# Two-layer decoder trunk on one core: the last two experts' rows spread over the tokens by TensorE instead of stored and loaded again

## The reference

```python
h = rms_norm(x, norm_ffn_w[layer])
# router: the best of 4 groups, then the best 2 of its 4 experts; weights e_w
gates = sum(one_hot(expert_id, 16) * e_w)            # 2 of 16 are non-zero per token
gu = einsum('nd,edf->nef', xt, w_gate_up)            # 16 experts, 1024 x 512
act = silu(gate) * up * gates
x = x + einsum('nef,efd->nd', act, w_down)           # 256 x 1024
```

## Time and profile before

| | us |
|---|---|
| runs | 1179.62, 1181.15, 1185.16 (median 1181.15) |
| profiled execution, its own time | 1181.09 |
| profiled execution, span | 1179.3 |
| PE busy | 1111.8 (94%) |
| DVE busy | 701.5 (59%) |
| ACT busy | 608.6 (52%) |
| POOL busy | 405.1 (34%) |
| DMA bytes | 194.76 MB, mean 165 GB/s |

### The profile page before, as it was taken

The page is one execution under the profiler, slowest core; times in us unless marked ns, Lnnn a source line. Parts: engine busy times, 40 slices in busy tenths (PEclk is TensorE's granted clock), DMA queues, the critical chain, the costliest instruction groups (busy, mean ns, idle before and its releaser), DMA issues.

```text
span 1179.3 us, 19724 instructions
## 1 busy us (share of the span) xinstructions
PE 1111.8 (94%) x7062; PEld 912.1 (77%) x7063; DVE 701.5 (59%) x1016; ACT 608.6 (52%) x903; POOL 405.1 (34%) x344
## 2 busy tenths in 40 slices
PE   8999999999998899998999999999999997999980
PEld 5778887778787688886788888888888886888870
DVE  5435444367736999996646341543442138999975
ACT  5556234242434699995633342233342234899871
POOL 4343121110133244442155325442244442344442
PEclk8999999999999899999999999999999997999995
DMA  9333311112225699996443213331222364999955
GB/s 262 79 86 56 72 38 55 37 44 66 72 68 210 244 353 375 379 364 238 174 128 98 81 56 106 97 106 56 81 73 91 104 190 161 354 388 374 358 208 223
DMA packets 89859, 194.76 MB, mean 165 GB/s; under 512 B 20348, under 2 KB 21432, under 8 KB 89016
## 3 DMA queue, kind: packets, MB, share of 16 engines
q1 hardware_dynamic: 67560, 159.34, 40.6%
q10 hardware_dynamic: 12432, 17.60, 4.4%
q0 software_dynamic: 9792, 16.80, 3.8%
HBM read 189.50 MB, written 23.07 MB: 180 GB/s over the span
## 4 chain that ended last, share of the span: by engine, by line
PE 80%; DVE 8%; DMA 5%; ACT 3%; issue 2%; ACTq 1%; SPq 0%; POOL 0%; POOLq 0%; DVEq 0%
PE ps L674 23%; PE ps L676 22%; PE ps L675 22%; PE ps L2570 2%; PE ps L2362 2%; DMA raw<-in_moe_w_down_dram 1%; DMA arena<-y 1%; DVE x L1467 1%; PE ps L2245 1%; ACTq L1421 1%; PE ps L2498 1%; DMA arena<-hs,slot_rows 1%; PE ps L2199 1%; ACT wh L1007 1%; DMA y<-arena,cur_rows 1%
## 5 line engine op out<-in xcount | busy, mean ns | idle before, releaser
L841 POOL TENSOR_TENSOR wl<-raw,wh 128x1024 fp32r<-128x1024 f32 x94 | 228.6, 2440 | 380.5 <-ACT wh L1007 380.2
L674 PE MATMUL ps<-wh,hT_hi 128*128 128x512 f32 x864 | 346.7, 401 | 3.5 <-DVE hT_lo L1986 2.4
L676 PE MATMUL ps<-wh,hT_lo 128*128 128x512 f32 x864 | 337.9, 391 | 0.0
L675 PE MATMUL ps<-wl,hT_hi 128*128 128x512 f32 x864 | 337.2, 390 | 0.0
L1007 ACT ACTIVATE wh<-raw 128x1024 fp32r<-128x1024 f32 x116 | 122.4, 1068 | 212.6 <-PE ps L676 191.0
L674 PEld LDWEIGHTS ps<-wh,hT_hi 128*128 128x128 f32 x864 | 162.8, 188 | 39.1 <-issue 3.5
L676 PEld LDWEIGHTS ps<-wh,hT_lo 128*128 128x128 f32 x864 | 162.3, 188 | 34.6
L675 PEld LDWEIGHTS ps<-wl,hT_hi 128*128 128x128 f32 x864 | 162.8, 188 | 30.9
L674 PE MATMUL ps<-hT_hi,wh 128*128 128x512 f32 (+1 forms) x296 | 116.9, 395 | 2.1 <-DVE arena_rounded L1818 1.0
L1961 DVE TENSOR_TENSOR wl<-arena,wh 128x1024 fp32r<-128x1024 f32 x96 | 113.8, 1222 | 4.7 <-ACT wh L1294 3.1
L1961 DVE TENSOR_TENSOR wl<-raw,wh 128x1024 fp32r<-128x1024 f32 x92 | 109.5, 1223 | 8.2 <-ACT wh L1294 5.4
(11 more groups left out here) (331 smaller groups left out, 1576.8 us busy)
## 6 DMA issues: line engine op xcount, KB each, us to landing
raw<-in_moe_w_gate_up_dram SPq DMA_DIRECT2D x64, 512.0 KB, 11.5
arena<-in_moe_w_gate_up_dram SPq DMA_DIRECT2D x64, 512.0 KB, 10.5
raw<-in_odd_w_in_dram SPq DMA_DIRECT2D x48, 512.0 KB, 3.7
raw<-in_even_w_in_dram SPq DMA_DIRECT2D x32, 512.0 KB, 4.8
arena<-in_moe_w_down_dram SPq DMA_DIRECT2D x32, 512.0 KB, 11.7
raw<-in_moe_w_down_dram SPq DMA_DIRECT2D x32, 512.0 KB, 14.1
raw<-in_odd_w_out_dram SPq DMA_DIRECT2D x16, 512.0 KB, 3.6
arena<-y ACTq DMA_DIRECT2D x6, 1024.0 KB, 9.9
```

Source lines behind the costliest of these rows:

```text
L674: nc.tensor.matmul(dst, lh, rh, start=first, stop=False)
L675: nc.tensor.matmul(dst, lh, rl, start=False, stop=False)
L676: return nc.tensor.matmul(dst, ll, rh, start=False, stop=last)
L841: pool.tensor_tensor(columns_of(i, wl[:, i % NSPL, :, :]), raw_columns(i), columns_of(i, wh[:, i % NSPL, :, :]).bitcast(F32), ALU.subtract ...
```

## The change

The last two experts (14 and 15, `LAST = NE - 2`) are no longer scattered to `y2`. What changes, part by part:

- ACT multiplies their results by the slot's weight while it copies them out of PSUM (`late_hi`, rounded), DVE makes the low part (`late_low`), and PE adds them to token tiles with a 0/1 matrix per expert (`slot_token`, 128 slots x 512 tokens): 8 matmuls of 128 x 512 for each token tile (`late_rows`). DVE adds the PSUM result to `X` (`add_late`).
- The matrices are made on DVE after its part of expert 0 (`slot_tokens`, two instructions of 128 x 512), from numbers made at the end of `pair_weights` (five more small instructions).
- The slots' weights: ACT stores the pair weights to DRAM after expert 1 (`w_dram`, 512 runs of 8 bytes), POOL gathers them by slot with two indirect DMAs. POOL also scatters rows of zeros to the pair rows of experts 14 and 15, by two indirect DMAs, so that the combines can go on over all of `y2`, with those pairs' weight set to 0 (`w_early`). The four stand after the first two experts' turn on POOL (`late_experts`).
- The five loads of `y2` are issued by SP, behind the first four pieces of the next layer, as soon as expert 13's scatter has landed.
- Order in `norm(2)` and `norm(4)` on DVE: two combines of tile 0, `late_low` of expert 15, then combines and `add_late` alternate. In `norm(2)` the low parts of layer 1's first two pieces go to POOL, the two others come after `lo_tiles` of tile 0. `keep_busy` is gone from PE; `late_rows` stand in its place and between the tiles.
- One more memset of 128 x 1024 (`no_rows`) in `outnorm` of each layer.
- The overflow branch is adapted.

```diff
-    return i in DVE_LO or ... or first_piece(10) <= i < first_piece(10) + 4
+    return i in DVE_LO or ... or first_piece(10) + 2 <= i < first_piece(10) + 4
 # SP
+            def load_early_rows(l):
+                for q in range(2):
+                    sp.wait_ge(s_(f"y_stored{q}"), 112 * (l + 1))
+                sp.wait_ge(s_("late_ready"), 64 * (l + 1))
+                sp.wait_ge(s_("slot_token_made"), 2 * (l + 1))
+                ...
+                sp.dma_start(YP[0][:, 0, :], src[0][:, 0, :]).then_inc(s_("yp_loaded0"), 16)
+                sp.dma_start(YP[0][:, 1, :], src[0][:, 1, :]).then_inc(s_("yp_second0"), 16)
+                for T in range(1, NT):
+                    sp.dma_start(YP[T], src[T]).then_inc(s_(f"yp_loaded{T}"), 16)
             for i in range(after, after + 4):
                 load(i)
+            load_early_rows(0)
             overflow_sp(sp, 0)
-            sp.wait_ge(s_("yp_loaded3"), 16)
 # POOL, between two_experts(0) and the loop
+                def late_experts():
+                    pool.wait_ge(s_("w_stored"), 16 * (l + 1))
+                    for e in range(2):
+                        ... indirect_dma_start(out=w_slot[:, e:e + 1], in_=w_dram[l], by rows) -> late_ready
+                    for e in range(2):
+                        ... indirect_dma_start(out=y2_dram[l], by rows, in_=no_rows) -> late_ready
 # ACT
+                    if last and par == 1:
+                        hi(m + 6 * NE)
+                        hi(m + 6 * NE + 1)
                     act.wait_ge(s_("ysb_free"), E + 1)
+                        if last:
+                            act.activation(late_hi[:, par, c], ps[:, 2 + hf, :], ACT.Copy, scale=w_slot[:, par:par + 1])...
+                            continue
+                    if n == 1:
+                        act.wait_ge(s_("slot_token_made"), 2 * (l + 1))
+                        act.dma_start(w_dram[l] ..., v3(w12, 4)).then_inc(s_("w_stored"), 16)
-                for q in range(2):
-                    act.wait_ge(s_(f"y_stored{q}"), 128 * (l + 1))
-                act.dma_start(YP[:, 0, 0, :], src[0][:, 0, :])...   # and the four others
 # DVE
+            def late_low(l, e, hf):
+                stt(late_lo[:, e, c], ps[:, 2 + hf, :], w_slot[:, e:e + 1], late_hi[:, e, c].bitcast(F32), ALU.mult, ALU.subtract)
+            def add_late(l, T):
+                dve.wait_ge(s_("late_rows"), 4 * l + T + 1)
+                D(tt(v3(X[:, T, :], 2), v3(X[:, T, :], 2), ps[:, b:b + 2, :], ALU.add), s_(f"moe_added{l}"))
 # DVE, norm(2) and norm(4)
+                    combine(l, 0, 0)
+                    combine(l, 0, 1)
+                    late_low(l, 1, 0)
+                    late_low(l, 1, 1)
+                    combine(l, 1, 0)
+                    add_late(l, 0)
+                    combine(l, 1, 1)
+                    add_late(l, 1)
 # DVE, norm(2) from there
+                    lo_tiles(("hT", n, 0), 0)
                     for i in range(4):
                         lo(first_piece(10) + i)
+                    for T in range(1, NT):
+                        if T + 1 < NT:
+                            combine(0, T + 1, 0)
+                            combine(0, T + 1, 1)
+                            add_late(0, T + 1)
                         lo_tiles(("hT", n, T), T)
 # DVE, norm(4) from there
+                    for T in (2, 3):
                         for j in range(2):
                             combine(1, T, j)
+                        add_late(1, T)
+                        last(T - 2)
                     last(2)
 # DVE, outnorm
+                D(dve.memset(no_rows, 0.0))
 # DVE, end of pair_weights, and after expert 0
+                D(dve.memset(w_slot, 0.0))
+                D(ts(slotB, slotA, 1, None, ALU.logical_shift_right))
+                D(ts(w_early, slotB, LAST // 2, None, ALU.not_equal))
+                D(tt(w_early, w_early, w12, ALU.mult))
+                D(tt(token_at, idx[:, 0, LAST:NE] ..., offs16[:, 0:NT] ..., ALU.subtract))
+            def slot_tokens():
+                for e in range(2):
+                    D(tt(v3(slot_token[e], NT), iotaB ..., token_at[:, e, :] ..., ALU.is_equal), s_("slot_token_made"))
 # DVE, end of expert 14 and 15
+                    if last:
+                        late_low(l, 0, par)
 # PE
+            def late_rows(l, T):
+                if T == 0:
+                    pe.wait_ge(s_("slot_token_made"), 2 * (l + 1))
+                elif T > 1:
+                    pe.wait_ge(s_(f"moe_added{l}"), T - l)
+                for e in range(2):
+                    pe.wait_ge(s_("late_low_made"), 4 * l + 2 * e + 2)
+                    for hf in range(2):
+                        mm(ps[:, b + hf, :], slot_token[e][:, cols(T)], late_hi[:, e, c], start=e == 0, stop=False)
+                        ins = mm(ps[:, b + hf, :], slot_token[e][:, cols(T)], late_lo[:, e, c], start=False, stop=e == 1)
             def norm(n):
                 if n == 2:
-                    keep_busy(22)
+                    late_rows(0, 0)
+                    late_rows(0, 1)
                 for T in range(NT):
+                    if n == 2 and T == 1:
+                        late_rows(0, 2)
...
-                            keep_busy(3)
                             rows(MOE_AT[0], T - 2, (3,))
+                        if T == 2:
+                            late_rows(0, 3)
 # PE, expert 15's down product; and step norm(4), which PE had nothing in
+                        if last and par == 1:
+                            pe.wait_ge(s_("late_low_made"), 4 * l + hf + 1)
+                    for T in range(NT):
+                        late_rows(1, T)
```

More of the change, by code:

```diff
@@ L347, in build @@
         vec = sb("vec", [P, 60])
-        small = sb("small", [P, 420])
+        small = sb("small", [P, 440])
         wba_h = sb("wba_hi", [P, KD, 8], F32R)
         wba_l = sb("wba_lo", [P, KD, 8], F32R)
+        with nc.sbuf_tensor("slot_token", [P, 1024], F32R) as tokens:
+            pass
         S = sb("state", [P, 512])
@@ L731, in build, with late_banks @@
         w12 = small[:, 404:412]
+        w_early, w_slot, token_at = small[:, 420:428], small[:, 428:430], v3(small[:, 430:438], 2)
+        def late_banks(l, T):
+            return 0 if T == 0 or (l == 1 and T == 2) else 2
         def overflow_flag(eng, l):
@@ L1320, in moe @@
                     expert(NE // 2 - 1, par)
-                for i in range(4):
+                for i in range(2, 4):
                     hi(m + 6 * NE + i)
@@ L1755, in lo @@
             def lo(i):
+                if not lo_by_dve(i):
+                    return
                 dve.wait_ge(hi_done, i + 1)
@@ L2693, in _ @@
                     norm(step[1])
+                elif k == "norm":
+                    for T in range(NT):
+                        late_rows(1, T)
                 elif k == "xT":
```

148 lines of the change are left out of this document (90 added, 58 removed).

## The result

1195.27 us, median of 4 runs (1192.22 to 1197.87), against 1180.38 (1179.56 to 1185.16) of 4 runs of the kernel before beside them: ratio 1.0117, 95% interval [1.0077, 1.0156]. The change makes the kernel slower, outside the range given. The profiled execution took 1197.87, 16.78 more than that of the kernel before (1181.09); its span is 1196.0.

What follows compares the result with a forecast made beforehand. PE was taken to set the pace, with 80% of the path and DVE, ACT and DMA close behind in the expert stage. 4.5 - 0.7 - 2.9 = 0.9 us gained, 1181.1 to 1180.2; range 1172 to 1187.

Steps and rivals of the forecast that it cites:

- Expert stage, per layer: Both layers' expert stages: 1.45 us lost per layer, 2.9 in both, bounds 0 and 4.8; all from DVE's inserts.
- the four small DMAs: POOL's four indirect DMAs in the expert stage: gather for expert 6 still in time, margin 2.5 us, cost 0.
- the 94%: Busy share of the DMA engines in layer 0's expert stage, where PE was said to set the pace.
- Rival (c): Expert stage: POOL's DMAs behind ACT's store make expert 6's gather late, about 4 us per layer, 1188.2 us; chance 0.13.
- Kernel's end: After the last expert: DVE's combines and adds finish earlier, 4.5 us gained, bounds 3 and 5.5.
- Between the layers: Handoff from layer 0 to layer 1: 0.7 us lost; by the bounds between 3.1 gained and 2.1 lost.
- POOL's lock: Between the layers: POOL's subtractions and DVE's combines wait for each other; without it the handoff comes out 2.4 us earlier.
- The clock: Between the layers: PE idles 5.5 us, then runs late_rows at half clock, 1.4 us late, bounds 0 and 2.8.
- DVE's inserts: First experts of each stage: five small instructions and two of 128 x 512 make PE 1.45 us late per layer.
- The memset in `outnorm`: In outnorm of each layer: hidden by POOL's lock in layer 0, by DVE's wait for PE in layer 1; 0.

Runs made afterwards that it cites:

- b_store8: Kernel before plus ACT's store of the weights alone, 512 runs of 8 bytes after expert 1: stage cost 3.2 us in layer 0, 1.3 in layer 1.
- v2: Changed kernel with zero rows, store and its gathers earlier, DVE's small instructions spread, its two products behind expert 15: handoff 64.6 us, expert 5 +0.8 and +1.1.
- v4: v2 with the first two low parts of the next layer back on DVE, no POOL subtractions between the layers: handoff 64.6 us, as in v2.
- b_inserts: Kernel before plus DVE's seven new instructions of the expert stage alone, results unread: PE 1.55 us late at expert 3 in layer 0, 1.54 in layer 1.
- b_store32: As b_store8 against the kernel before, but the same 4 KB in 128 runs of 32 bytes: cost the stage nothing.
- b_all: Kernel before plus everything new of the expert stage and the second outnorm memset, without the changed stage ends: stages 14.1 us longer.

## Why the prediction was wrong

The failed step is the last of "Expert stage, per layer": that the zero rows "now fall into the stage with 94% DMA; PE's own lateness gives the time back: 0", and with it the 0 for the four small DMAs. That put 0 where 5.5 and 4.2 us stood between experts 6 and 15, plus 0.9 and 1.4 at expert 6: 12.0 us of the two stages' 15.1, where 2.9 were forecast. The mechanism behind it was wrong, not only the size: I took PE for the pace-setter with its own margin per instruction, and read the 94% as load. PE's lateness gives nothing back, since SP's next load waits for DVE's low part of an earlier one, and DVE goes with PE from piece to piece: a late PE asks for its pieces later, too. SP's wait in the kernel before, from 430 to 540 us:

```profile
SPq L801 <- DVE wl L1961: 50.1, 53, 2.2
```

The row that would have told it was in the trace of the kernel before: the time to landing of its loads, 7.0 us early in the stage and 15.0 near its end. A queue that grows all through a stage is one that is fed faster than it drains.

Rival (c) named the place (POOL behind ACT's store) and the sign, at 0.13, but its 4 us per layer were to come from expert 6's gather. That cost 0.9 and 1.4; the same store cost more by what it did to the loads (3.2 and 1.3 in b_store8, which has no such wait).

Point by point:
- Kernel's end: 4.5 gained forecast, 4.2 measured from the last copy to DVE's end. The first combine came at 1167.72, 15.4 us after expert 15's transposes, forecast 16.1; the halved clock, counted nothing here, held DVE's first two adds up by 0.58 and 0.46 us.
- Between the layers: 0.7 lost forecast, 1.2 measured, which is within the spread of executions. That the start of the combines came out right (19.7 us after expert 15's transposes, forecast 19.1) is luck. The forecast had it wait for POOL's lock, with the load there 2.4 us earlier. In fact the load landed 3.0 us later than counted, and the lock did not bind: POOL ended 0.65 us ahead of the load. v2 and v4 show that it exists (products 3.47 against 1.41 us, POOL 5.70 against 4.73). The clock did bind, as forecast: DVE's first add waited 1.04 us for products at half clock.
- DVE's inserts: 1.45 per layer up to expert 3 forecast, 1.5 measured, alone (b_inserts) and in the changed kernel.
- The memset in `outnorm`: 0 forecast. In layer 0 its time vanished in the lock ahead of the casts (from its start to DVE's first add 6.88 us, before, from the start of the next memset, 6.94). Of the 3.5 us up to expert 1, some come from TensorE at 1.2 GHz in the router (its 24 products took 4.10 instead of 2.87 us). They aren't the memset's: b_store32, which lacks it, is as late there, and b_all, which has it, is 1.45 us earlier than the kernel before.
- Open too: why 0.5 MB of zero rows cost 3.8 us alone, where their bytes are 1.4. From 440 to 530 us the loads ran at 367 GB/s instead of 374, some 1.7 us of supply. They did so before PE was late, too (370 against 378 from 440 to 490), and b_store8 has the same, 368 against 375 of b_store32. What slows them no run tested.

## What to carry to other kernels

Where a stage loads nearly as fast as it computes, read the loads' time from issue to landing at its beginning and at its end: if it grows, the stage lives on stock, and a transfer added after the last moment with full slots is paid at its end (here 0.5 MB cost more than its bytes), while the same one well ahead of that moment was free. Moving it is of use only if it also lands ahead of that moment. Count a small store not by its bytes or its own landing but by its runs, for the loads beside it pay. And ahead of a wait of some microseconds on PE, price the matmuls behind it at half clock, or keep PE busy by a number of instructions read from a row.

## What the runs showed of the hardware that was not expected

- 512 runs of 8 bytes (4 KB) held the loads beside them at 77 to 229 GB/s for 5 us; with 128 runs of 32 bytes it was 235 to 351.
- A copy of 4 MB within DRAM, issued in eight parts from 69 to 122 us, where the DMA engines had been 27 to 63% busy, cost PE about 4 us, 1.7 to 2.8 of them in one wait of the kind "issue" and much of the rest at half clock behind it. What it waited for, no row says.
- A DVE product of 128 x 512 with both inputs in SBUF took 1.74 us beside POOL's subtractions (3.47 for two) and 0.71 without.
